# The norm seams between GEMM stages in three token tiles, with the neighbouring units of both GEMMs run tile by tile

## What is computed

```python
def rms_norm(x, w):
    return x * lax.rsqrt(jnp.mean(x * x, axis=-1, keepdims=True) + 1e-6) * w

for layer in range(2):
    h = rms_norm(x, norm_mix_pre[layer])
    if layer == 0:
        u, q, k, v = split(h @ w_in_even)             # 1280 columns
        mix = concat(s5_mixer(u), attention(q, k, v)) @ w_out_even
    else:
        q, fz, iv, gz = split(h @ w_in_odd)           # 4096 columns
        mix = hgrn2_mixer(q, fz, iv, gz) @ w_out_odd
    x = x + rms_norm(mix, norm_mix_post[layer])
    h = rms_norm(x, norm_mlp_pre[layer])
    h = square(relu(h @ w_up[layer])) @ w_down[layer]  # 4096 wide
    x = x + rms_norm(h, norm_mlp_post[layer])
```

## Time and profile before

| What | Value |
|---|---|
| Runs | 3086.34 us median of 3 (3079.87 to 3093.56) |
| The profiled execution, its own time | 3095.64 us |
| its span, first to last instruction | 3093.8 us, 40686 instructions |
| mean granted clock of TensorE | 0.925 of full |
| TensorE busy | 2764.8 us (89%) |
| VectorE busy | 1500.2 us (48%) |
| ScalarE busy | 551.3 us (18%) |
| GpSimd busy | 1020.7 us (33%) |
| DMA | 223.48 MB, mean 72 GB/s |

### The profile page before, as it was taken

The page is one execution under the profiler, slowest core; times in us unless marked ns, Lnnn a source line. Parts: engine busy times, 40 slices in busy tenths (PEclk is TensorE's granted clock), DMA queues, the critical chain, the costliest instruction groups (busy, mean ns, idle before and its releaser), DMA issues.

```text
span 3093.8 us, 40686 instructions
## 1 busy us (share of the span) xinstructions
PE 2764.8 (89%) x16759; PEld 2621.2 (85%) x16759; DVE 1500.2 (48%) x1390; ACT 551.3 (18%) x699; POOL 1020.7 (33%) x432
## 2 busy tenths in 40 slices
PE   8958578979999999997899999996969999999995
PEld 6956447968999999995898989985859999999994
DVE  4924364372443334446366666667364333334336
ACT  3000163030000000003233333334130000000001
POOL 2314001358566656643000000000343434433444
PEclk9976568989999999998999999998989999999997
DMA  3151202116233322232211111120201111111111
GB/s 130 41 86 45 58 0 77 48 77 224 103 108 109 122 108 102 102 116 83 89 69 51 70 70 70 59 73 15 97 21 42 48 48 45 43 47 41 47 47 56
DMA packets 85554, 223.48 MB, mean 72 GB/s; under 512 B 22535, under 2 KB 33832, under 8 KB 85304
## 3 DMA queue, kind: packets, MB, share of 16 engines
q1 hardware_dynamic: 45504, 165.70, 15.3%
q10 hardware_dynamic: 39944, 56.31, 5.9%
HBM read 163.34 MB, written 58.61 MB: 72 GB/s over the span
## 4 chain that ended last, share of the span: by engine, by line
PE 59%; DVE 10%; ACT 3%; issue 2%; DMA 0%; DVEq 0%; POOL 0%; ACTq 0%; SPq 0%; POOLq 0%
PE ps L295 42%; PE ps L1472 7%; PE ps L1531 3%; PE ps L304 3%; DVE lev L1597 2%; ACT lev L1724 2%; DVE h_lo L533 2%; DVE x L408 2%; PE ps L319 1%; PE ps L1571 1%; DVE ssq L513 1%; DVE ck L1597 1%; DVE cum L1597 1%; DVE raw L1597 1%; PE ps L1550 0%
## 5 line engine op out<-in xcount | busy, mean ns | idle before, releaser
L218 POOL TENSOR_TENSOR w_hi<-w_raw,ones 128x1024 fp32r<-128x1024 f32 x156 | 300.6, 1927 | 1899.0 <-PE ps L295 1022.9
L295 PE MATMUL ps<-a_hi,w_hi 128*128 128x352 f32 x2064 | 670.0, 325 | 14.7 <-DVE q_t L827 6.4
L295 PE MATMUL ps<-a_hi,w_lo 128*128 128x352 f32 x2064 | 666.4, 323 | 0.0
L295 PE MATMUL ps<-a_lo,w_hi 128*128 128x352 f32 x2064 | 665.2, 322 | 0.0
L220 POOL TENSOR_TENSOR w_lo<-w_raw,w_hi 128x1024 fp32r<-128x1024 f32 x156 | 437.3, 2803 | 12.2
L295 PEld LDWEIGHTS ps<-a_hi,w_hi 128*128 128x128 f32 x2064 | 389.8, 189 | 15.9 <-DVE q_t L827 6.6
L295 PEld LDWEIGHTS ps<-a_lo,w_hi 128*128 128x128 f32 x2064 | 392.0, 190 | 0.0
L295 PEld LDWEIGHTS ps<-a_hi,w_lo 128*128 128x128 f32 x2064 | 389.7, 189 | 0.0
L295 PE MATMUL ps<-h_hi,w_hi 128*128 128x352 f32 x1152 | 374.9, 325 | 4.0 <-POOL w_lo L220 3.9
L295 PE MATMUL ps<-h_hi,w_lo 128*128 128x352 f32 x1152 | 371.4, 322 | 0.0
L295 PE MATMUL ps<-h_lo,w_hi 128*128 128x352 f32 x1152 | 370.6, 322 | 0.0
(11 more groups left out here) (274 smaller groups left out, 4103.4 us busy)
## 6 DMA issues: line engine op xcount, KB each, us to landing
w_raw<-w SPq DMA_DIRECT2D x156, 512.0 KB, 3.7
p_raw<-w SPq DMA_DIRECT2D x32, 512.0 KB, 4.5
w_hi_scratch<-p_hi SPq DMA_DIRECT2D x32, 512.0 KB, 2.7
w_lo_scratch<-p_lo SPq DMA_DIRECT2D x32, 512.0 KB, 3.5
w_hi<-w_hi_scratch SPq DMA_DIRECT2D x32, 512.0 KB, 3.8
w_lo<-w_lo_scratch SPq DMA_DIRECT2D x32, 512.0 KB, 4.7
x<-x ACTq DMA_DIRECT2D x16, 528.0 KB, 7.5
x_scratch<-x ACTq DMA_DIRECT2D x16, 528.0 KB, 2.7
```

The source lines that it names most:

```text
L218: pool.tensor_tensor(hi, w_raw[:, b, :], ones[:, 0:1].broadcast_to([P, KC * P]), ALU.mult).then_inc(hi_made, 1)
L295: mm = pe.matmul(tiles[:, t], wt[:, b, w], at_[:, k, cols], start=(n == 0 and i == 0), stop=(n == len(ks) - 1 and i == 2))
```

## The change

Boundary is written anew; all its steps run on one tile of 352 tokens at a time (tile 0, then 1, then 2, eight k in each). The last n units of the GEMM before (n = 4 in the MLPs, 2 in the projections) and the first two units of the GEMM behind run tile by tile too. TensorE's order is: the n items of tile 0; those of tile 1, with the post-norm statistic of tile 0 in the middle; those of tile 2; the statistic of tile 1; then for tile 0 the eight pre-norm statistics with unit 0's products, the post-norm statistic of tile 2, unit 1's products; and the same for tiles 1 and 2. Banks 0 to 5 take the items by turns, and then unit 0 (banks 0 to 2) and unit 1 (3 to 5); banks 6 and 7 take statistics.

GpSimd no longer scales y: VectorE does it. The mean is folded into Ln's scale and bias (eps), read from PSUM; the table is loaded once in each boundary, at its start. sq has four slots of one tile for x and two for y. Weights of the tiled last units go to other places, so that the next stage's first two blocks can be split in the usual slots: `spare` (columns 704 to 959 of a_hi and a_lo) in an MLP's last group, `alt` (in the space of h_lo) in a projection. For this all splits write three-dimensional views, and w_hi's second operand is ones[:, 0:128] repeated for eight k. x comes in 16 pieces in load; y leaves in 24; x is saved to x_scratch with tile 2. In the heads tiles n = 3 to 5 of head 0 (unit 1) have moved into the boundary. eps has an address of its own and is set at the start.

```diff
+            def spare(n):
+                c = 2 * TT + n * P
+                return a_hi[:, :, c:c + P], a_lo[:, :, c:c + P]
...
-            hi, lo = (w[:, b].rearrange("p k m -> p (k m)") for w in (w_hi, w_lo))
-            pool.tensor_tensor(hi, w_raw[:, b, :], ones[:, 0:1].broadcast_to([P, KC * P]), ALU.mult).then_inc(hi_made, 1)
+            hi, lo = halves or (w_hi[:, b], w_lo[:, b])
+            whole = w_raw[:, b, :].rearrange("p (k m) -> p k m", m=P)
+            pool.tensor_tensor(hi, whole, bc(ones[:, 0:P], 1, KC), ALU.mult).then_inc(hi_made, 1)
...
+                    def last_group():
+                        for j in range(6):
+                            block_of(GROUPS - 1, j)
+                        for j in (6, 7):
+                            block_of(GROUPS - 1, j, HID, spare(j - 6))
...
-                        block_of(0, j)
+                        block_of(0, j, (-3, -2)[j] if j < 2 else None)
...
+            def pe_tail(self, pe):
+                n = self.source.n
+                for i in range(n):
+                    self.pe_item(pe, 0, i)
+                for i in range(n):
+                    if i == n // 2:
+                        self.pe_stat_y(pe, 0)
+                    self.pe_item(pe, 1, i)
+                for i in range(n):
+                    self.pe_item(pe, 2, i)
+                self.pe_stat_y(pe, 1)
...
+                for t in range(3):
+                    done = unit_done if t == 2 else tile_ready
+                    if t == 1 and self.post is not None:
+                        pe.wait_ge(*self.ln_y(3))
+                    elif t == 2:
+                        pe.wait_ge(*self.ln_x(1))
+                    for k in range(KC):
+                        s = t * KC + k
+                        pe.wait_ge(*self.squared_x(s + 1))
+                        pe.matmul(ps[:, self.STAT_X[t], 0:TT], ones[:], sq_slot(s % 4), start=(k == 0),
+                                  stop=(k == KC - 1)).then_inc(self.stat_x.sem, 1)
...
+                        pe.wait_ge(*self.lo(s + 1))
+                        products(0, t, k, t, done)
+                    if t == 0:
+                        if self.post is not None:
+                            self.pe_stat_y(pe, 2)
+                        weights_ready(pe, 1)
+                    if self.post is not None:
+                        pe.wait_ge(*self.taken(3 * self.source.n - 3 + t + 1))
+                    for k in range(KC):
+                        products(1, 3 + t, k, t, done)
...
+            def vector(self, dve, x_ready=None):
+                late = {}
+                if self.post is not None:
+                    n = self.source.n
+                    early, rest = range(n // 2), range(n // 2, n)
+                    self.vec_items(dve, 0, range(n))
+                    self.vec_items(dve, 1, early)
+                    late = {1: (1, rest), 4: (2, early), 6: (2, rest)}
+                for s in range(3 * KC):
+                    t, k = divmod(s, KC)
+                    if k == 0:
+                        if s and self.pre is not None:
+                            self.vec_lo(dve, s - 1)
+                        if self.post is not None:
+                            self.vec_scaled(dve, s)
...
+                    if self.post is not None:
+                        if k + 1 < KC:
+                            self.vec_scaled(dve, s + 1)
+                        dve.wait_ge(*self.scaled(s + 1))
+                        dve.scalar_tensor_tensor(x[:, k, tile(t)], y[:, k, tile(t)], gains[:, self.post, k:k + 1],
+                                                 x[:, k, tile(t)], ALU.mult, ALU.add).then_inc(self.x_made.sem, 1)
+                    if k and self.pre is not None:
+                        self.vec_lo(dve, s - 1)
+                    if s in late:
+                        for i in late[s][1]:
+                            self.vec_take(dve, late[s][0], i)
...
+            def act_rsqrt(self, act, t, bank, ready, ln, rstd_done):
+                act.wait_ge(*ready)
+                act.activation(rstd[:, tile(t)], ps[:, bank, 0:TT], ACT.Ln, scale=1.0 / D, bias=eps[:, 0:1]).then_inc(ln.sem, 1)
+                act.wait_ge(*ln(t + 1))
+                act.activation(rstd[:, tile(t)], rstd[:, tile(t)], ACT.Exp, scale=-0.5).then_inc(rstd_done.sem, 1)
...
+                    squares = {1: (1, rest), 4: (2, early), 6: (2, rest)}
+                    rsqrt_y = {5: 1, 10: 2}
+                if self.pre is not None:
+                    rsqrt_x = {14: 0, 20: 1, 23: 2}
...
-            for n in range(3, 12):
+            for n in range(6, 12):
-                pe_head_tile(pe, 0, n)
+                pe_head_tile(pe, 0, n, free=f"t{n - 6}" if n < 9 else None)
...
-            load.act.wait(act, "rstd_x")
+            act.wait_ge(*load.rstd_x(3))
+            act.wait_ge(*load.lo(3 * KC))
             act_s5_loads(act)
```

More of the change, by code:

```diff
@@ L307, in pe_share, with pe_first_unit, pe_projection @@
                 mm.then_inc(unit_done, 1)
-        def pe_first_unit(pe, name, tile_done=None):
+        def pe_first_unit(pe, name):
             def part(k):
-                if k == 0 and name == AHEAD:
-                    pe.wait_ge(w_whole[0], 32)
-                elif k == 0:
+                if k == 0:
                     pe.wait_ge(w_ready, FIRST_SPLIT[name] + 1 + LOOKBACK)
[L316 to L322, removed]
-            return part
-        def pe_projection(pe, name, evacuated, started=False):
-            n0, nb = FIRST_SPLIT[name], dict((s[0], s[1]) for s in STREAM)[name]
+                pe_share(pe, 0, 0, k, KC, (a_hi, a_lo), k, k == KC - 1)
+            return part
+        def pe_projection(pe, name, evacuated, first, count):
+            n0 = FIRST_SPLIT[name]
             def one(i, b):
@@ L392, in vector @@
-            def vector(self, dve, x_ready=None):
-                v = self.vec
-                v.prime(dve)
-                if self.post is not None:
-                    dve.wait_ge(self.stat_y, 1)
-                    v.done(dve.tensor_scalar(t3(ssq[:]), unit(0), 1.0 / D, EPS, ALU.mult, ALU.add), "mean_y")
-                    self.act.wait(dve, "rstd_y")
-                for k in range(KC):
+                self.tag, self.post, self.pre, self.source = tag, post, pre, None
+                at_ = ("load", "mix0", "mlp0_end", "mix1", "mlp1_end").index(tag)
@@ L410, in vector @@
-                    if self.pre is not None and k > 0:
-                        self.lo(dve, k - 1)
-                if self.pre is not None:
-                    self.lo(dve, KC - 1)
-                    dve.wait_ge(self.stat_x, KC)
-                    v.done(dve.tensor_scalar(t3(ssq[:]), unit(1), 1.0 / D, EPS, ALU.mult, ALU.add), "mean_x")
-            def pool(self, pool):
-                self.act.wait(pool, "rstd_y")
-                for k in range(1, KC):
-                    pool.tensor_tensor(y[:, k], y[:, k], rstd[:], ALU.mult).then_inc(self.scaled, 1)
@@ L519, in vec_group @@
                 self.lo(dve, g, HID - 1)
-                for m in range(KC):
-                    dve.wait_ge(unit_done, self.units(HID + m, g))
+                for m in range(HID if last else KC):
+                    dve.wait_ge(unit_done, self.units_of(HID + m, g))
                     v.wait_last(dve, g)
@@ L1897, in _ @@
             pool.wait_ge(ones_set, 1)
-            pool_weights(pool, {"glu": StatesOnPool(), "mlp0": mix0, "in_odd": end0, "mlp1": mix1})
-            end1.pool(pool)
+            pool_weights(pool, {"glu": StatesOnPool()})
         @block.tensor
@@ L1944, in _ @@
             vec_lower_bound(dve)
[L1945 removed]
+            dve.wait_ge(*end0.rstd_x(3))
             he.prime(dve)
```

431 lines of the change are left out of this document (256 added, 175 removed).

## The result

The changed kernel takes 3009.73 us (median of 4 runs, 3008.23 to 3010.51) against 3087.64 us (4 runs, 3079.87 to 3093.56): ratio 0.975, 95% interval 0.973 to 0.977. Forecast: 2998 us, 2972 to 3030. It is faster, inside the range, 12 us above the point.

A forecast was written before the change was run, and what follows sets the result against it. TensorE's waits in five seams bound the kernel. 28.2+28.2+31.6+18.1-6.3-8.0-2.5-1.0 = 88.3 us gained: span 3093.8 becomes 3005.5, own time 3007.3, median 9.3 lower, 2998 us; range 2972 to 3030.

The forecast's parts named there:

- the last one: From own time 3007.3 us to the median of the runs: taken as 9.3 us below the profiled execution, 2998.
- the later S5: After x's loading: S5 starts 6.3 us later behind a later rstd; seven splits beside its preparation lose 2.5 us.
- the MLPs: In the 16 MLP groups: slower w_hi lies on the path, 0.5 us each, 8.0 us lost.
- end1: Last seam, to the span's end: from 64.4 to 46.3 us, 18.1 us gained.
- TensorE's work and its end in the mix seams: Seams mix0 and mix1: 62.0 us of TensorE work plus 1.5 wait, 63.5 instead of 91.7; 28.2 gained twice.
- end0: Seam before the heads: TensorE restarts after 71.0 us instead of 91.1, one more unit done; 31.6 us gained.
- load: Seam where x is loaded: more products precede the last statistic, so rstd and S5 come later; 6.3 us lost.
- The operand: Weights' split on GpSimd: w_hi goes from 1.90 to 2.40 us; 8.0, 2.5 and 1.0 us lost.
- A: Rival, weights' split: the new operand costs nothing and 11.5 us come back, 2986 us; chance 0.25.
- B: Rival, seams: VectorE paces, by full durations +10 us (3008) or at 0.68 us each +42 (3040); 0.12 for both.
- C: Rival, four seams: TensorE pays for each turn from ones-matmuls to products, 17 us, 3015; chance 0.10.
- D: Rival, GpSimd: three-dimensional w_hi far slower, using up the gain at 6.2 us each, kernel slower than before; chance 0.02.

The follow-up runs named there:

- bf_full: The kernel before with only the new w_hi operand and the three-dimensional views of the split: 3103.17 us, ratio 1.004.
- e1: The changed kernel with w_hi's second operand back to one held column of ones, three-dimensional views kept: 2994.07 us, ratio 0.967.
- e2: The changed kernel with unit 1's products issued after the last statistic, only in the boundary where x is loaded: 3005.08 us, ratio 0.971.
- e3: The changed kernel with the held column for w_hi and, at the loading of x, unit 1's products behind the last statistic: 2984.61 us, ratio 0.965.
- e4: The changed kernel with unit 1's products issued behind the last statistic in every boundary: 3002.97 us, ratio 0.971.
- e5: The changed kernel with the 24 scalings of y per boundary on GpSimd, tile by tile, not on VectorE: 3023.66 us, ratio 0.978.
- e6: The changed kernel with held column, late unit 1 products at x's loading, and masks and reset loads right behind the last x save: 2977.05 us, ratio 0.963.
- b1_before: The kernel before, unchanged, in one more profiled execution: 3091.85 us, span 3090.0.

## Why the prediction was right, and where it missed

**The step that failed is the last one**, from the execution to the median. Span: forecast 3005.5, measured 3007.5; own time 3007.3 against 3009.57. Then the prediction took 9.3 us off for the median, as in the kernel before, and the changed kernel's median is 3009.73, its own execution's time. A profiled execution is one draw. Profiled less median, in the order before, bf_full, after, e1, e2, e3, e4, e5, e6: +9.3, +1.3, -0.2, +0.5, +4.6, +10.0, -1.8, -0.4, -1.8 us. The offset isn't a property of the kernel or of profiling: part of before's was its slow attention, 8.6 us more than in b1_before. With none taken off the forecast would have missed by 2.4 us. That closeness is in part luck. Against the trace of b1_before the span fell by 82.5 us, not 86.3; and of the terms, the later S5 and the MLPs cost more than forecast, while end1 and a shorter attention gave back about as much (below).

**TensorE's work and its end in the mix seams, right.** Forecast 62.0 us of work, measured 62.00 busy; 63.5 to unit 2, measured 64.06. The pause before block 2 is 2.06, not 1.5: w_lo ran beside VectorE's 1056-wide passes and took 3.26 us. T0 to the last a_lo: forecast 55.3, measured 646.91+0.58-593.01 = 54.5.

**end0, right in size and in what is late next.** Gained 31.4 (forecast 31.6; against b1_before's seam it would be 33.6); restart at T0+72.1 (71.0), idle 9.90 (9), and the first matmul again 0.63 us. The masks load took 6.3 us from its issue to the cast (issued at 1442.58), with SP's scratch loads issued at 1439.92 and 1443.79 beside it; the prediction had said that these cost nothing, and that isn't settled.

**end1, 2.1 us better.** 44.2 against 46.3. VectorE's starts are 0.43 to 0.50 us apart (rows above), not all 0.50, and its last operation ends at T0+41.9 instead of 43.3; the last output piece lands 2.3 us behind it, not 3.

**load, right in sign and near in size.** rstd 7.2 us later (6.3), S5's first operation at 63.58 (near 63). S5 itself starts 11.8 us later than in the first profile of before and 7.9 than in the second; forecast 6.3+2.5 = 8.8. Both named causes are real, but they don't add. rstd is first used at 57.5 to 58.6 in the three kernels that have unit 1's products in front of the last statistic, and at 49.4 to 50.4 in the four of the new form that don't. S5 starts at 181.20 in the changed kernel, at 176.15 with the held column alone (e1_held), at 173.24 with the late products alone (e2_load) and at 172.01 with both (e3_both), which lies between the two executions of before (169.43 and 173.35). Of the 11.8 us only 5.6 are left at mix0's T0, and that is luck: the attention of this execution took 166.2 us, 6.6 less than that of before, and b1_before shows such differences without any change. What the prediction left out is that the unit behind waits as well (11.34 us, 4.36 before): u_p comes late, while the splits of the next blocks run on GpSimd from 57.70 to 67.5.

**The operand, right in mechanism, too small in size.** w_hi 2.40 as forecast, h_lo 1.1 as forecast; priced at 11.5, it cost 13.5 and 15.7 us. Missing were the waits for w_lo in group 0 of mlp0 (1.9 us). For 2.8 us of the operand's share in the MLPs, and for the 2.3 of 15.2 us that stay with the held column, the cause is open; the pace (below) may be part of both.
The Trainium skill (GPSIMD Engine Reference, section 2.1 Instruction dispatch) puts every two-input operation at about 2.5 cycles an element; bf_full and e1_held, on either side of the change of operand, show 2.40 and 1.89 us for the same 1024 elements a partition. The prediction's estimate from the Trainium skill's figures was 2.1 us or more, so this rule doesn't hold for a held column.

**Rivals.** A (the operand is free) is refuted by bf_full and e1_held. B (VectorE paces) by its 47.81 busy of 64 us and by its starts: operations that the rows show as 0.52 and 0.58 long start 0.43 and 0.49 apart. By the Trainium skill (VectorE: DVE Perf Modes, The DRAIN you can't avoid) a start waits for the pipe to empty, but the same section lets an operation that is not held start earlier, which the prediction left out. The rows overlap by 0.09 us and so go with that exception. C (a price for each turn) is refuted by tile 1 of mix0: a statistic with its three products takes 1.07 us from start to start. Three such steps, with a turn in each, are 3.21 us; the old cycle of the same three statistics and nine products, with one turn, took 3.23. So a turn costs nothing. TensorE's timeline, two steps:
```profile
619.15 0.75 PE L449 MATMUL ps<-sq,ones 128*128 128x352 f32 x2
...
620.22 0.75 PE L449 MATMUL ps<-sq,ones 128*128 128x352 f32 x2
...
621.29 0.75 PE L449 MATMUL ps<-sq,ones 128*128 128x352 f32 x2
```
D (w_hi over 6.2 us) never came near: the longest of 148 took 4.55.

## What to carry to other kernels

A norm between two GEMMs need not empty TensorE: cut the norm and the last units before it by token tiles, so that the first tile's norm begins while the others are still multiplied, and count TensorE's own work in the seam; once the vector engine fits inside that count, the seam is as long as the count, and a finer order of the products brings little (e4_defer). A small edit that rides along, here the operand of the split, is priced on the path of the steady loop, not in the seam it came with. And don't carry the distance between one profiled execution and the median over to another kernel.

## What the runs showed of the hardware that was not expected

GpSimd multiplies [128, 1024] by one held column in 1.893 us and by a [128, 128] operand read eight times in 2.401; three dimensions or two make no difference.

Small operations of VectorE on two SBUF operands take 0.58 us alone and 1.26 while GpSimd runs a scaling of the same size, which takes 1.18 itself.

The matmul pace has a second value that the granted clock doesn't show. Two neighbouring groups of mlp1 in the changed kernel, with the same instructions at a clock of 1.00:
```profile
2474.24:2567.73 93.49, 92.44 (x577) 91.58 (x577) 35.41 (x21) 4.36 (x4) 41.98 (x16) 1.00 0.14 45
2567.73:2662.30 94.57, 93.48 (x576) 92.62 (x576) 35.44 (x21) 4.35 (x4) 41.98 (x16) 1.00 0.13 44
```
Units of the projections show it too: 11.44, 11.52 or 11.60 us apart in mix1, by execution. What sets it stayed open; it is worth 1.2% in these two groups and up to 1.4% in the units, and it bounds what a difference of a few us between two profiles can tell.
